# A triangular solve on TensorE: the lower factor's products in four 32x32 diagonal tiles instead of two 64x64 block-diagonal ones

## What is computed

```python
def _rwkv7_scan(r, w, k, v, za, zb):
    def step(S, inp):
        r_t, w_t, k_t, v_t, a_t, b_t = inp
        sa = jnp.einsum("bhij,bhj->bhi", S, a_t)
        S = S * w_t[:, :, None, :] + sa[..., None] * b_t[:, :, None, :] + v_t[..., None] * k_t[:, :, None, :]
        return S, jnp.einsum("bhij,bhj->bhi", S, r_t)
    ...
    _, ys = lax.scan(step, S0, xs)
```

## Time and profile before

| | us |
|---|---|
| median of 3 runs | 743.42 |
| the three runs | 742.17, 743.42, 743.67 |
| span of the profiled execution | 741.7 |
| TensorE busy in the span | 730.6 |
| VectorE busy | 576.3 |
| ScalarE busy | 435.5 |
| GpSimd busy | 47.1 |

### The profile page before, as it was taken

How to read it: one execution, slowest core, us unless ns; L and a number is a source line. 1 busy time by engine, 2 the same in 40 slices (tenths; PEclk the granted TensorE clock), 3 DMA queues, 4 the chain that set the end, 5 groups by cost and what they waited for, 6 DMA issues and landing times.

```text
span 741.7 us, 16496 instructions
## 1 busy us (share of the span) xinstructions
PE 730.6 (98%) x7072; PEld 597.3 (81%) x7072; DVE 576.3 (78%) x908; ACT 435.5 (59%) x679; POOL 47.1 (6%) x81
## 2 busy tenths in 40 slices
PE   9999999999999999999999999999999999999997
PEld 6888877889778888888877686898888888865553
DVE  5899976777889999998678887899786666762444
ACT  5699872523656766666656573487584655653342
POOL 0000133040020000000002000003003000000000
PEclk9999999999999999999999999999999999999999
DMA  9990303512574566557690743339326165566001
GB/s 316 395 401 5 114 17 139 206 38 81 179 275 146 196 228 224 177 175 253 240 353 1 266 189 114 115 114 340 116 89 252 48 241 174 221 227 219 37 0 58
DMA packets 67146, 129.43 MB, mean 174 GB/s; under 512 B 3969, under 2 KB 28033, under 8 KB 66817
## 3 DMA queue, kind: packets, MB, share of 16 engines
q1 hardware_dynamic: 66032, 126.07, 47.2%
q0 software_dynamic: 320, 1.61, 0.6%
q10 hardware_dynamic: 720, 0.70, 0.3%
HBM read 127.32 MB, written 1.05 MB: 173 GB/s over the span
## 4 chain that ended last, share of the span: by engine, by line
PE 78%; DVE 12%; ACT 4%; DMA 4%; issue 1%; SPq 0%; DVEq 0%; ACTq 0%
PE bank L623 35%; PE bank L3218 11%; PE bank L739 11%; DVE arena L569 3%; PE bank L2540 3%; DMA ring<-in_w_in_dram 2%; PE bank L1551 2%; PE bank L874 1%; PE bank L1570 1%; PE bank L1832 1%; DMA ring<-in_ffn_w_up_dram 1%; PE bank L893 1%; DVE arena L1076 1%; PE bank L1885 1%; PE bank L2012 1%
## 5 line engine op out<-in xcount | busy, mean ns | idle before, releaser
L623 PE MATMUL bank<-hg,arena 128*128 128x256 f16 x2496 | 275.4, 273 | 1.5 <-DVE arena L556 1.1
L623 PEld LDWEIGHTS bank<-hg,arena 128*128 128x128 f16 x2496 | 243.6, 98 | 32.6 <-issue 2.6
L569 DVE SCALAR_TENSOR_TENSOR arena<-ring,arena 128x1024 f16<-128x1024 f32 x150 | 175.5, 1227 | 52.7 <-ACT arena L537 52.7
L537 ACT ACTIVATE arena<-ring 128x1024 f16<-128x1024 f32 x150 | 146.6, 1044 | 83.8 <-PE bank L3218 37.6
L3218 PE MATMUL bank<-arena 128*128 128x512 f16 (+1 forms) x480 | 83.6, 336 | 0.0
L3218 PEld LDWEIGHTS bank<-arena 128*128 128x128 f16 x480 | 47.0, 98 | 36.1
L739 PE MATMUL bank<-arena 128*128 128x256 f16 x528 | 57.8, 273 | 0.0
L739 PEld LDWEIGHTS bank<-arena 128*128 128x128 f16 x528 | 51.7, 98 | 6.0
L556 DVE SCALAR_TENSOR_TENSOR arena<-ring,arena 128x2048 f16<-128x2048 f32 x22 | 50.4, 2292 | 0.7
L739 PE MATMUL bank<-mix,arena 128*128 128x256 f16 x384 | 42.2, 273 | 0.0
L549 ACT ACTIVATE arena<-ring 128x2048 f16<-128x2048 f32 x22 | 41.7, 1895 | 0.0
(11 more groups left out here) (425 smaller groups left out, 992.5 us busy)
## 6 DMA issues: line engine op xcount, KB each, us to landing
ring<-in_w_in_dram SPq DMA_DIRECT2D x12, 2048.0 KB, 9.7
ring<-in_ffn_w_up_dram SPq DMA_DIRECT2D x22, 1024.0 KB, 7.8
ring<-in_w_ff_dram SPq DMA_DIRECT2D x8, 2048.0 KB, 8.9
ring<-in_w_ff_dram SPq DMA_DIRECT2D x16, 1024.0 KB, 6.6
ring<-in_ffn_w_down_dram SPq DMA_DIRECT2D x11, 1024.0 KB, 6.6
ring<-in_w_out_dram SPq DMA_DIRECT2D x8, 1024.0 KB, 7.7
ring<-in_w_xk_dram SPq DMA_DIRECT2D x2, 2048.0 KB, 11.8
ring<-in_w_xv_dram SPq DMA_DIRECT2D x2, 2048.0 KB, 10.3
```

The costliest lines, as they stand in the source:

```text
L537: nc.scalar.activation(quarter(halves_of(chunk)[0], chunk, q), quarter(slot(*chunk), chunk, q), ACT.Copy, scale=W_SCALE).then_inc(*mark("w ...
L569: nc.vector.scalar_tensor_tensor(quarter(halves_of(chunk)[1], chunk, q), quarter(slot(*chunk), chunk, q), W_SCALE, quarter(halves_of(chunk ...
L623: mm = nc.tensor.matmul(out_, weight[a][:, k, cols], src[:, k, b, :], start=(first and i == 0), stop=(last and i == 2), skip_group_check=True)
```

## The change

The stationary operand of the lower factor's products becomes `LT32`: the raw blocks times -1, as they lie in the bank, 128 partitions by 4 heads by 32 columns. It takes one VectorE instruction per chunk and group that reads 128x128 and writes 128x128, where the old one wrote 128x256 and read a constant too. The products then go to four 32x32 tiles on the array's diagonal, like the inverse's products, where they went to two 64x64 tiles: 16 products per level and group instead of 8, each over 32 rows instead of 64, with the same 16 moving columns. The constant `blocks64` goes out of the table, which becomes 64 columns narrower. Nothing else changes, and no engine's order does. Lines behind the change move up by 1 to 6.

```diff
-    ("blocks64", 2 * BASE),
...
-    put("blocks64", (np.arange(2 * BASE)[None, :] // BASE == r // BASE % 2) * -1.0)
...
-        LT64 = [view(SOLVE + 3104 + 512 * g, 4, 2 * BASE) for g in range(2)]
+        LT32 = [view(SOLVE + 3104 + 512 * g, 4, BASE) for g in range(2)]
...
                     for j in range(4):
-                        for i in range(2):
-                            q = slice(64 * i, 64 * i + 64)
-                            mm = nc.tensor.matmul(banks[3 * g][q, half * j:half * j + half], LT64[g][q, j, :],
+                        for b in range(4):
+                            q = slice(BASE * b, BASE * b + BASE)
+                            mm = nc.tensor.matmul(banks[3 * g][q, half * j:half * j + half], LT32[g][q, j, :],
                                                   even(st["X"][q, j, :], m), start=True, stop=True,
-                                                  tile_position=(64 * i, 64 * i))
+                                                  tile_position=(BASE * b, BASE * b))
                     mm.then_inc(*mark("solve_pe", "P bank", c, g, n))
...
-                nc.vector.tensor_tensor(
-                    LT64[g].rearrange("p j (two n) -> p j two n", two=2),
-                    blocks.unsqueeze(2).broadcast_to([P, 4, 2, BASE]),
-                    const("blocks64").rearrange("p (two n) -> p two n", two=2).unsqueeze(1).broadcast_to(
-                        [P, 4, 2, BASE]), ALU.mult).then_inc(*mark("solve_vector"))
+                nc.vector.tensor_scalar(LT32[g], blocks, -1.0, None, ALU.mult).then_inc(*mark("solve_vector"))
```

## The result

| | before | after |
|---|---|---|
| median, us (6 runs each, on one chip) | 742.91 | 746.55 |
| lowest to highest, us | 742.17 to 744.00 | 744.91 to 749.46 |
| span of the profiled execution, us | 741.7 | 744.9 |

The ratio of after to before is 1.0044 with an interval of 1.0031 to 1.0058: 3.6 us more at the medians, and outside the predicted range.

The account below looks back on a forecast made before the run. TensorE, busy 98% of the span, was taken as the bound where others wait for it, chiefly in the solve. 0.47 + 0.36 + 0.38 + 0.38 = 1.59 us off the median 743.42 gave 741.8 us, range 740.2 to 743.0.

Parts of the forecast that it names:

- First chunk, level 0: First level of the solve: shorter copies and shorter products both on the path, together 0.47 us gained, between 0.22 and 0.55.
- First chunk, levels 1 and 2: Level 1: nothing, masks wait behind VectorE's gate work; level 2: SSD rates start 0.36 us earlier, between 0.25 and 0.38.
- Second chunk, level 0: TensorE's own queue is full there, so shorter loads move the rest up: 0.38 us gained, between 0.3 and 0.4.
- Second chunk, levels 1 to 3: Levels 1 and 2: nothing, masks wait behind VectorE work; level 3: VectorE idle, 0.38 us gained, between 0.3 and 0.45.
- Products: Lower factor's products, every solve level: loads fall from 1.01 to 0.63 us, 0.38 less; 3.0 us over eight levels before waits.
- a gain lost behind the solve: Closing sign: if all four steps show but the time does not, the transfer behind the solve was misread.
- Rival 3: Lower factor's products cost 32 ns each however small, 2.05 us per level instead of 1.01: 748.2 us, slower; chance 0.03.
- Rival 4: More clock falls at covered levels where TensorE idles 0.38 us longer, 1.3 us each; two give 744.4 us; chance 0.07.
- Rival 1: The first chunk's clock fall goes away in most executions, saving 1.3 us more: 740.5 us; chance 0.13.
- The sixteen products of a single column: First chunk, thin TensorE work ahead of level 2's products and the clock's fall; unchanged, so the fall was expected to stay.
- The fills: Twelve full products at each level that stay where they are, cited against further clock falls in the second chunk.
- K: Theory of the experiments, not of the prediction: only stretches at the lower clock make the difference.

Follow-up runs that it names:

- The first chunk alone: Four 32x32 tiles and the compact copy in the first chunk only, second chunk as in the kernel before: 742.40 us, ratio 0.9987; repeated, 742.12 us.
- the count taken away: Changed kernel, but in the second chunk one 32-column product serves two heads, so odd heads are solved wrongly and instructions are as few as before: 741.69 us, ratio 0.9972.
- the count put in beside old products: Kernel before, plus 8 unread four-band 32x32 products per level and group beside the second chunk's inverse products: 747.80 us, ratio 1.0062.
- the first padding: Kernel before, plus 8 unread 32x32 products on two bands ahead of the old ones, per level and group of the second chunk: 749.22 us.
- the version with level 0: Kernel before, with the new products in the first chunk and at the second chunk's level 0 only: 741.03 us, ratio 0.9967; repeated, 740.25 us, ratio 0.9963.

## Why the prediction was wrong

The forecast started from 743.42, the median of three runs. Six give 742.91, from which the same sum makes 741.3, so the base hides 0.5 us of the miss. The steps:

- *First chunk, level 0*: 0.47 worked, 0.46 found. The copy takes 0.28 us and not 0.24, and the mask's wait is 0.46 after 0.64.
- *First chunk, levels 1 and 2*: nothing and 0.36 worked, nothing more and 0.36 found. The first chunk alone is 0.9 us faster, where its steps sum to 0.83.
- *Second chunk, level 0*: 0.38 worked and found.
- *Second chunk, levels 1 to 3*: wrong. The holes stand here. The step that failed is the price under *Products*: "Per level 32 instructions at 1.01 us become 64 at 0.63 us". The load's time is right, 0.63, but it is the time of instructions that are there. The count leaves out the product behind each load (64 instructions become 128), and nothing was priced for the arrival of 512 more in the whole kernel, 256 of them in this chunk, and the second chunk's levels had no slack for them: 65 instructions per us asked before, 64 to 75 supplied (256 in 3.4 to 4.0 us). In the first chunk, one-column products, gate products and waits stretch the levels, so the same addition fits but for the 0.29 us at level 0. The loss stands inside the solve, so what the prediction would have concluded last, a gain lost behind the solve, is not what happened.
- *A sign of it was on the page*: 56 instruction transfers and 0.92 MB, and the number of instructions per level in the timeline. The prediction used the first nowhere. How fast the transfers can come the page does not say; before, they came 3.4 to 4.7 us apart in the second chunk.
- *Rival 3* had the right sign and the right noun, instructions, but the wrong mechanism and place: no product takes longer (10 ns a load), and the cost is a hole elsewhere in the stream, at times in the fill or in the inverse's products.
- *Rival 4* came in as a consequence: a fall in the second chunk, but one of 6.8 us and not two of 3.4, behind holes and not behind covered levels. *Rival 1* came in for the one profiled execution of after, whose first chunk kept the full clock. (The sixteen products of a single column that the prediction names ahead of the fall are sixteen product instructions, of eight products.)
- The fills, named as what would keep the clock up, are themselves part of the stream that ran late.

That the holes are the supply is shown: by the count of 128 loads between them, by the count taken away (741.69) and by the count put in beside old products (747.80). In the last the padding's own time and the clock add to the holes, so it is the trace and not the time that shows it. K fails as the sole cause, since the holes are in the rows ahead of the fall. Whether they bring the fall on was not shown: it stands at or right behind them in four kernels, but the first padding has it at the same place without a hole, and no run separated the two.

The Trainium skill (Runtime: NRT & Kernel Launch, Instruction fetch mechanics) says that instructions are refilled in blocks of 16 KiB, 256 instructions, and that crossing into the next block is mostly hidden. The rows agree with the block: 128 loads and 128 products at a time. They disagree with the second part: 2.09 to 2.85 us stood open at each block in the dense products, 3.99 us in all in the changed kernel, and the measurement decides.

## What to carry to other kernels

Before cutting products into smaller tiles, count the instructions of the stretch and divide by its length: here TensorE got about 256 per 3.4 to 4.0 us, and a gain in time per product was worth only what this leaves. A run of equal instructions that breaks in the middle with "issue" as the reason, and breaks that lie a constant count apart, are the sign of it. Put a change that adds instructions only into stages with slack, as the version with level 0 does, or halve the count again with wider moving operands, where products share a stationary operand (the heads here do not).

## What the runs showed of the hardware that was not expected

- TensorE's instructions come in transfers of 256, at best one per 3.4 to 4.0 us in these stretches; after a stretch that asks for less, some 223 loads with their products were in store.
- Four diagonal 32x32 tiles on four bands take 10 ns a load, two bands 21 ns. Per band that is 40 and 42 ns: here the band's own time is the price, not the instruction's.
- 512 loads of 64x64 with products of 16 columns kept the row PE fully busy, and the granted clock still stood at 0.50 for 22 of their 25 us.
